# Cumulated forget gates of a forgetting attention, spread over the partitions by six transfers and joined with the mask on GpSimd, in place of six-row products on TensorE

## The reference

```python
log_f = jax.nn.log_sigmoid(fl.astype(jnp.float32) + forget_bias[i].astype(jnp.float32))

def forgetting_attention(q, k, v, log_f):
    c = jnp.cumsum(log_f.astype(jnp.float32), axis=1).transpose(0, 2, 1)
    ...
        s = jnp.einsum('bhqd,bhkd->bhqk', qb.astype(jnp.float32), k32) * scale
        s = s + cb[..., None] - c[:, :, None, :]
        s = jnp.where(pos[None, :] <= tq[:, None], s, -jnp.inf)
        p = jax.nn.softmax(s, axis=-1)
        return jnp.einsum('bhqk,bhkd->bhqd', p.astype(v.dtype), v)
```

## Time and profile before

| | |
|---|---|
| median of 3 runs | 914.55 us (914.38 to 915.19) |
| the profiled execution | 915.04 us, span in the trace 913.2 us |
| granted TensorE clock | 0.997 of full speed |
| PE | busy 886.5 us, 97% of the span |
| DVE | 597.2 us, 65% |
| ACT | 466.2 us, 51% |
| POOL | 95.1 us, 10% |
| transfers | 152.64 MB, mean 167 GB/s |

### The profile page before, as it was taken

One profiled execution on the slowest core, in us unless ns is written; L12 is line 12 of the kernel. 1 busy time (PEld: TensorE's weight loads), 2 busy tenths in 40 slices (PEclk: granted clock), 3 DMA queues, 4 the chain that ended last, 5 costly groups with the idle time before them and its releaser, 6 DMA issues.

```text
span 913.2 us, 19495 instructions
## 1 busy us (share of the span) xinstructions
PE 886.5 (97%) x7408; PEld 852.9 (93%) x7408; DVE 597.2 (65%) x967; ACT 466.2 (51%) x742; POOL 95.1 (10%) x149
## 2 busy tenths in 40 slices
PE   8999999999999989999999999999998999999997
PEld 8988899999999989778899999999898899999996
DVE  5676567665665676547676666668879866666665
ACT  6546765443444465337644444445786644444443
POOL 3320002000000019600100000001140100000000
PEclk9999999999999999999999999999999999999999
DMA  7532246556556647523455555554435455555551
GB/s 260 164 116 93 94 162 219 184 174 203 180 172 204 185 140 215 165 93 108 171 173 188 187 187 184 186 185 159 158 101 192 149 186 184 184 184 184 186 182 47
DMA packets 44948, 152.64 MB, mean 167 GB/s; under 512 B 5861, under 2 KB 7141, under 8 KB 44901
## 3 DMA queue, kind: packets, MB, share of 16 engines
q1 hardware_dynamic: 41184, 145.52, 48.6%
q0 software_dynamic: 2912, 5.48, 1.8%
q10 hardware_dynamic: 804, 0.98, 0.3%
HBM read 148.58 MB, written 1.05 MB: 164 GB/s over the span
## 4 chain that ended last, share of the span: by engine, by line
PE 88%; DVE 7%; ACT 2%; issue 1%; DMA 1%; SPq 0%; DVEq 0%; POOL 0%; ACTq 0%
PE bank L1239 27%; PE bank L1241 26%; PE bank L1240 26%; DVE alo L867 3%; PE bank L1588 2%; PE bank L1329 1%; DVE h L877 1%; DVE wlo L842 1%; PE bank L1274 1%; PE bank L1679 1%; PE bank L1346 1%; DMA raw<-in_slabs 1%; PE bank L1369 1%; ACT whi L467 1%; DVE sq L1172 1%
## 5 line engine op out<-in xcount | busy, mean ns | idle before, releaser
L1239 PE MATMUL bank<-ahi,whi 128*128 128x256 f32 (+1 forms) x1400 | 400.3, 286 | 5.3 <-DVE proj L886 2.9
L1241 PE MATMUL bank<-ahi,wlo 128*128 128x256 f32 (+1 forms) x1400 | 393.5, 281 | 0.0
L1240 PE MATMUL bank<-alo,whi 128*128 128x256 f32 (+1 forms) x1400 | 393.1, 281 | 0.0
L842 DVE TENSOR_TENSOR wlo<-raw,whi 128x1024 fp32r<-128x1024 f32 x273 | 333.8, 1231 | 31.2 <-ACT whi L467 30.9
L467 ACT ACTIVATE whi<-raw 128x1024 fp32r<-128x1024 f32 x273 | 282.3, 1051 | 104.4 <-PE bank L1241 99.6
L1239 PEld LDWEIGHTS bank<-ahi,whi 128*128 128x128 f32 x1400 | 263.8, 188 | 8.8 <-DVE proj L886 3.5
L1240 PEld LDWEIGHTS bank<-alo,whi 128*128 128x128 f32 x1400 | 263.9, 188 | 0.5
L1241 PEld LDWEIGHTS bank<-ahi,wlo 128*128 128x128 f32 x1400 | 264.0, 189 | 0.0
L1239 PE MATMUL bank<-hidhi,whi 128*128 128x256 f32 x704 | 198.1, 281 | 3.0 <-issue 2.1
L1240 PE MATMUL bank<-hidlo,whi 128*128 128x256 f32 x704 | 197.6, 281 | 0.0
L1241 PE MATMUL bank<-hidhi,wlo 128*128 128x256 f32 x704 | 197.5, 281 | 0.0
(11 more groups left out here) (208 smaller groups left out, 696.2 us busy)
## 6 DMA issues: line engine op xcount, KB each, us to landing
raw<-in_slabs SPq DMA_DIRECT2D x273, 512.0 KB, 3.4
shared<-zpad POOLq DMA_DIRECT2D x64, 35.5 KB, 3.1
shared<-in_convw POOLq DMA_DIRECT2D x4, 512.0 KB, 6.3
raw<-in_slabs SPq DMA_DIRECT2D x8, 128.0 KB, 5.7
vtok<-in_gatew POOLq DMA_DIRECT2D x2, 512.0 KB, 4.2
out<-y SPq DMA_DIRECT2D x4, 256.0 KB, 2.7
h<-in_xT ACTq DMA_DIRECT2D x3, 272.0 KB, 5.5
h<-in_xT SPq DMA_DIRECT2D x1, 272.0 KB, 3.2
```

The source lines that it names most:

```text
L842: dve.tensor_tensor(wlo[:, n % R, :, :], raw[:, n % R, :, :], whi[:, n % R, :, :].bitcast(F32), ALU.subtract).then_inc(lo_done, 1)
L1239: pe.matmul(dst, hi, xh, start=start, stop=False, skip_group_check=True)
L1240: pe.matmul(dst, hi, xl, start=False, stop=False, skip_group_check=True)
L1241: return pe.matmul(dst, lo, xh, start=False, stop=stop, skip_group_check=True)
```

## The change

The running sum is no longer subtracted by PE. ACT starts six transfers, one for each head; each reads the one row of `cum` 128 times and writes it to all 128 partitions (into `fgate[1]`, which lies in `t8`, a buffer with no use at that time). For each head, when its transfer has landed, POOL makes mask minus row for the 144 keys of the first query block (`fgate[0]`) and for the 272 of the second (`fgate[1]`, in place). DVE's `fox_bias` adds this in place of the mask alone, after a wait for `gate_mask`. The constant `nsel` and its three instructions on POOL go. DVE makes the running sum one column earlier.

```diff
-        nsel = first_only(FL_P, FOX_HEADS, P)
+        fgate = [first_only(P, FOX_HEADS, FOX_N[0]),
+                 t8[:, :, :].rearrange("p a b -> p (a b)")[:, 0:FOX_HEADS * T1].rearrange("p (a b) -> p a b", a=FOX_HEADS)]
...
-        consts_done = 13
+        consts_done = 12
...
-            step(pool.memset(nsel[:, :, :], 0.0))
-            step(pool.affine_select(out=nsel[:, :, :], in_=nsel[:, :, :], compare_op=ALU.not_equal, fill=-1.0, base=0,
-                                    pattern=[[-1, FOX_HEADS], [0, P]], channel_multiplier=1))
-            select(nsel[:, :, :], ALU.not_equal, -1.0, -HD, [[-1, FOX_HEADS], [0, P]], 1)
...
+            for hd in range(FOX_HEADS):
+                pool.wait_ge(gate_spread[hd], 16)
+                for t in range(2):
+                    m = FOX_N[t]
+                    pool.tensor_tensor(fgate[t][:, hd, :], fmask[:, t, 0:m], fgate[1][:, hd, 0:m], ALU.subtract)\
+                        .then_inc(gate_mask, 1)
+                    pool.wait_ge(gate_mask, 2 * hd + t + 1)
...
+            act.wait_ge(cum_ready, 1)
+            for hd in range(FOX_HEADS):
+                act.dma_start(fgate[1][:, hd, :], cum[hd:hd + 1, :].rearrange("p (a n) -> p a n", a=1).broadcast_to([1, P, T1])).then_inc(gate_spread[hd], 16)
             act.wait_ge(consts, consts_done)
             act.activation(tri_r[:, :], tri[:, :], ACT.Copy).then_inc(sb_ones, 1)
...
-                if n == IN1 + 5:
+                if n == IN1 + 4:
                     dve.wait_ge(fl_ln, 1)
...
+                dve.wait_ge(gate_mask, 4 * (s // 2) + 2 * hd + t + 1)
+                return dve.scalar_tensor_tensor(dst, acc_bank[hd][:, 0:n], cumT[:, c:c + 1], fgate[t][:, 2 * (s // 2) + hd, :],
                                                 ALU.add, ALU.add)
...
-            def forgetting(pair, hd, dst, n):
-                b = HD * hd
-                return pe.matmul(dst, nsel[b:b + FOX_HEADS, 2 * pair + hd, :], cum[b:b + FOX_HEADS, 0:n], start=False, stop=True)
...
-                    pair_scores(s, 0, QF, KF, 0, FOX_N, acc_bank[0:2], forgetting)
+                    pair_scores(s, 0, QF, KF, 0, FOX_N, acc_bank[0:2])
```

## The result

The changed kernel took **933.84 us** (median of 4 runs, 933.40 to 934.34), the kernel before 914.63 (4 runs, 914.38 to 915.19) beside it: ratio 1.0208, 95% interval 1.0196 to 1.0220. It is slower, as forecast, but by 19.2 us and not by 10.75, and outside the range. Its profiled execution took 933.53 us, span 931.7, granted clock 0.988.

A forecast was written before the change was run, and what follows sets the result against it. PE, busy 97% of the span, was taken to bound the kernel. PE 11.85 us late at the mixer, less 0.45 and 0.66 in steps 4 and 5, made +10.75; with the median 0.5 lower, 925.3 us, range 912.6 to 928.5.

The forecast's parts named there:

- What bounds the kernel, and what the removal is worth: PE's stream sets the time; leaving out the six pairs of products removes 3.3 us of PE, at most 2.7 gained.
- Step 3's share: The 0.66 us of PE products removed in step 3 gain nothing, since PE waits there for DVE at the mixer products.
- step 5's 0.66: Removing PE's products of line 1401 in step 5 was to give back 0.66 us.
- What ACT has to do more: Six transfer starts on ACT at 0.47 us delay the copies of the values; PE's column of slot 1 comes 0.87 us late.
- d = 5.1 us: Time for one row's spread to 128 partitions, 139,264 bytes read from one partition, taken at one DMA engine's stream rate.
- The rival at full width: Each row is read by sixteen engines at once, 0.47 us a spread; only ACT's delay stays: -1.35 us, 913.2 us; chance 0.28.
- Heads 4 and 5 don't queue: Their rows land with head 3's at 56, so only step 0's wait counts: +5.2, 919.8 us; chance 0.16.
- Slabs starve: The spreads hold the DMA engines 30 us; if slabs come late, 1 to 4 us more; chance 0.1.
- (1): Step 0: DVE's bias of head 1 waits for its first mask, ready at 46.55; PE's transposes come 6.8 us late.
- (3): Mixer: POOL's windowed sums stand behind the last mask and end at 73.85; PE's mixer products come 11.85 us late.

The follow-up runs named there:

- transfers_alone: The kernel before, products and masks kept, with ACT's six one-partition transfers added and nobody waiting for their landing before 130 us: 935.38 us against 914.96, ratio 1.0230.
- two_alone: The kernel before with only the transfers of heads 0 and 1 added on ACT, without a reader: 914.73 us in one execution, against 914.59.
- sixteen_sources: The changed kernel with each head's running sum on sixteen partitions, each read 8 times, still started by ACT: 915.86 us against 914.96, ratio 1.0010.
- pool_start: The changed kernel with its six one-partition transfers started by POOL, two at first and others after masks, none by ACT: 924.87 us against 914.92, ratio 1.0109.
- sixteen_pool_start: The changed kernel with the running sum on sixteen partitions and all six transfers started at once by POOL: 912.60 us against 914.92, ratio 0.9976.

## Why the prediction was wrong

**What bounds the kernel, and what the removal is worth: right.** At most 2.7 us were named; 2.0 was measured without anything in the products' place, 2.3 in the best version. Step 3's share was worth nothing, as said, and step 5's 0.66 only some 0.3.

**Failed: "What ACT has to do more".** It priced six starts at 0.47 us, 2.8 in all, and so made the copies of the values 1.3 us late and the column of slot 1 only 0.87. The starts held ACT for 21.7 us, and that column came 18.5 us late. The row behind the price, three starts of 1.42 us, was of starts on an empty queue of fast transfers. The prediction had the number that spoke against it in hand: six transfers of 5.1 us each, started within 2.8 us. It asked who waits for the landing, and never asked what a start costs while the transfers ahead of it are under way. By transfers_alone this one term is the whole loss; two_alone shows that it isn't there for two transfers, and sixteen_sources that it goes when the reads are fast (0.61 to 0.79 us a start). A smaller error in this step hid itself: the starts do not wait for the slab rounding to end (the first stands at 32.61, beside the rounding of 32.59), and cost 0.61 to 0.79 us each even when fast, so that sixteen_sources came out at exactly the 0.87 us of delay, by 4.1 us of starts from 32.6 in place of 2.8 from 33.9.

**d = 5.1 us: right in size, in part by luck.** The landings lay within 1.4 us of the six predicted, and the reads took some 5.4 us each. But the first row landed 8.0 us after its start and not 6.8, and the start came 1.3 us earlier than forecast: two errors that cancel. And 5.1 was worked out as the stream of one DMA engine. The trace shows the packets of ACT's queue taking 77% of the time of all sixteen, while four sources that lie apart gave 64 GB/s in 20.5% of it: the source partition set the rate, not one engine's stream. (Nor did the rows that reached hundreds of GB/s have 128 partitions "at both ends": they came from the kernel's inputs in memory.) The rival at full width fell. "Heads 4 and 5 don't queue" held in part. From 54 to 56 us the changed kernel's queue moved 0.11 MB:

```profile
q10 hardware_dynamic: 117, 0.11, 81.6%
```

That is 55 GB/s, twice the 26 GB/s that one partition gave, so head 4's row seems to have been read beside head 3's. But head 4's start had ended only at 48.5, and it landed 5.7 us after head 3; head 5 came 2.6 us behind it. "Slabs starve" didn't happen in PE's waits.

**(1) and (3), the two waits behind the masks: right mechanism, hidden here.** DVE waited 9.7 us for masks, but PE was held elsewhere until 55.76, long after step 0's masks of both heads (41.2 and 47.0). The larger delay covers the smaller. Moved out from under it (pool_start), both waits came up, at 924.87 us. The masks themselves took 0.49 and 0.76 us, less than the 0.65 and 1.2 taken.

**Not priced at all: the clock.** The column after the long wait took 5.0 us in place of 3.2, most of it at a granted clock of 0.50. The sum counted a wait of PE at its length only; here it is 1.8 us more.

**The range.** Its upper end, 928.5, came from d and from starved slabs; no bound was given for a start, though the trace of before showed none behind slow transfers. A bound lay near, seen afterwards: if two starts are taken and each of the other four waits for one transfer, the hold is an estimated 4 x 5.1 = 20.4 us, of the 21.7 measured.

## What to carry to other kernels

Price a transfer twice: its landing, for whoever waits on it, and its start, for whatever stands behind it on the engine that starts it. Here a start was cheap (0.55 to 0.8 us) for two slow transfers and for six fast ones, and dear for six slow ones, so slow transfers belong on an engine with nothing urgent behind them, or must be made fast first. When one row is to be spread by transfer, first have it computed on partitions that lie apart (here free, by repeated weight columns), and then start it from the engine that will read it.

## What was not expected of the hardware

- A start instruction held ACT's whole stream while earlier slow transfers were under way: 0.55 and 0.66 us for the first two, 3.41 for the third, then 5.56 to 5.80, about the time of one transfer. The activations behind it stood still, and the list of waits calls it "issue".
- Reading one partition 128 times took some 5.4 us for 139,264 bytes, four neighbours 6.1 us, four partitions 8 apart 2.2 us.
- TensorE's clock fell to its 1.2 GHz level (0.50) after PE stood idle: idle from 36.6, a mean of 0.66 from 38 to 42, 0.50 from 42 to 58, and full speed again from 62 (0.78 between), with PE at work from 55.76.
- POOL's masks and DVE's slab difference lengthen each other when they lie side by side: in sixteen_pool_start a mask of 144 columns took 1.36 us in place of 0.50, and the slab difference beside it 1.74 in place of 1.22.
